# A transformer block in one kernel: four FFN halves computed inside the output projection, and a reordered compression

## The chip, the cores and the metric

The program runs on one core of one Trainium2 chip. The metric is the device time in microseconds, here the median of three runs. One further execution was taken by the hardware profiler, and all rows below are of that one.

## What is computed

One layer on 2048 tokens of width 1024: a mixer with three kinds of attention (one of them with compressed keys and values), an output projection, and a gated FFN with a short convolution. The parts that the change touches:

```python
def compress(a, pos, w1, b1, w2):            # a: keys or values, n T G hd
    ch = a.reshape(n, T // CMP_STRIDE, CMP_STRIDE, G, hd)
    blocks = jnp.concatenate([ch[:, j:j + nc] for j in range(n_sub)], axis=2)
    blocks = blocks + pos[None, None, :, None, :]
    flat = blocks.transpose(0, 1, 3, 2, 4).reshape(n, nc, G, CMP_LEN * hd)
    return jax.nn.gelu(flat @ w1 + b1) @ w2

mix = jnp.concatenate([o_a, o_b, o_c], axis=-1) @ w_out[l]
x = x + rmsnorm(mix, g_mix_post[l])
f = conv_glu_ffn(rmsnorm(x, g_ffn_pre[l]), w_up[l], conv_w[l], conv_b[l], w_down[l])
x = x + rmsnorm(f, g_ffn_post[l])

def conv_glu_ffn(h, w_up, conv_w, conv_b, w_down):
    u = causal_conv3(h @ w_up, conv_w) + conv_b      # per channel, 3 taps
    a, b = jnp.split(u, 2, axis=-1)
    return (jax.nn.gelu(a, approximate=True) * b) @ w_down
```

(`causal_conv3` stands for the grouped convolution of the reference.)

## The kernel before

The kernel is written engine by engine: each stage is a block in which every engine has its own list of instructions, with semaphores between them, and a stage begins when all engines have ended the one before. The stages are `project` (the input projection), `compress`, `attend`, `mix_out` (the output projection) and `ffn`. Nothing is scheduled by a planner; the order on each engine is the order of the code.

Every float32 product is made of three: an operand is split into a high part (a copy in the type float32r, made by ScalarE) and a low part (the difference, made by VectorE or GpSimd), and high × high, low × high and high × low are summed in one PSUM bank.

`compress` (L546) does this for m = 0 (keys) and m = 1 (values), each with a 2048 × 256 weight in 16 chunks, in quarters of 4 chunks. ScalarE makes `x_hi` (L656) and then `w_hi` per quarter (L659). VectorE makes the small low parts of the positions (L693), then `x_lo` (L683), then the low part of the weights in place in `w_raw` (L687). TensorE (L620 to L637) waits for `x_lo` and the first quarter's low part and goes chunk by chunk, with all three products of a chunk for both column halves. GpSimd only clears three tiles.

`mix_out` (L1531) goes over 16 row blocks of 128 tokens. In step t TensorE transposes the attention output of row block t + 1 (`turn_o`, L1749, into the PSUM tile `t1`), multiplies row block t by the output weights (L1767, tile `mix`, two slots) and transposes the normalised rows `h2` of row block t − 1 (L1776, tile `t2`). The last step, t = 16, has only the transposes of row block 15. SyncE's queue serves this in one fixed order, per step: three pieces of the attention output for t + 2 (`load_o`, L1601 to L1603), after the row block's `x1` is done its store (L1622) and the load of x for s + 2 (L1624), after the split of `h2` its two stores (L1627). Steps 0 and 1 are written out, the rest stands in a hardware loop (`steps`, L1580). When four row blocks are stored, GpSimd loads the FFN's first activations `f_h` (L1649, two loads of 2048 KB). Before the steps, ScalarE, VectorE and GpSimd split the output weights (L1640, L1654), whose raw rows lie in tiles of the attention stage (`w_rows`).

`ffn` (L1790) goes over four quarters of 512 tokens. In each, 22 steps `up` (L1895) make two halves each (b = 0, 1), a half being 24 matmuls (L1909) into one bank; ScalarE (L1954, L1955, L1959, L1961) and VectorE (L1992 to L2007) convolve, apply gelu and split the result. Then 22 steps `down` (L1913, L1929) fill all eight banks, and the row blocks are normalised and stored (VectorE L2013, L2018, GpSimd L1855 to L1867). The weights, 66 pairs of 512 KB per quarter, pass through a ring of 6 slots (SyncE, L1845, L1846); a slot is loaded again when TensorE is done with it. `up` waits for its slot, and for the banks that ScalarE has to empty:

```python
pe.wait_ge(w_in[s % RING], q * (32 * (STEPS // RING)) + 32 * (s // RING) + 32)
if j < 2:
    pe.wait_ge(f_taken, q * TQ + j + 1)
else:
    pe.wait_ge(u_done, q * (2 * NF) + 2 * (j - 2) + b + 1)
    pe.wait_ge(acc0_done, q * (2 * NF) + 2 * (j - 2) + b + 1)
```

All quarters are one hardware loop on each of TensorE, ScalarE, VectorE and SyncE.

## Time and profile before

| | us |
|---|---|
| median of 3 runs (3561.64 to 3566.04) | 3562.96 |
| the profiled execution | 3558.06 |
| its span, first to last instruction | 3556.3 |

| engine | busy us | share of the span |
|---|---|---|
| TensorE, matmuls | 3398.8 | 96% |
| TensorE, weight loads | 2708.3 | 76% |
| VectorE | 1385.9 | 39% |
| ScalarE | 1161.9 | 33% |
| GpSimd | 559.2 | 16% |

The span is what lies between the first and the last instruction of the profiled execution; that execution's own time is 1.8 us longer. The mean granted TensorE clock is 0.981 of full speed. DMA moved 190 GB/s in the mean. By the stages that matter here, the compression's TensorE work lies at 804 to 832 us from the span's start, the output projection at 1823 to 2049, and the FFN from 2058 to the end. A matmul's busy time in the rows overlaps with the next one's, so durations of many matmuls are read from their starts. Between `<-` and the name in square brackets a row says what ended an engine's idle time; "issue" is time in which it waited for nothing that the profile shows.

### The profile page before, as it was taken

To read this page: it belongs to the slowest core of one execution; us is meant where nothing else is said; L and a number is where in the kernel's file an instruction comes from. 1 tells how busy PE (TensorE), PEld (TensorE's weight loads), DVE (VectorE), ACT (ScalarE), POOL (GpSimd) and SP (SyncE) were. 2 spreads that over 40 slices of the span, in tenths; PEclk is the share of its full clock that TensorE was granted. 3 is DMA by queue.
4 is the path that set the end of the run, shared out by engine and by line. 5 is a ranking of instruction groups with operands and counts; after the bars stand their busy time and mean duration, and the time that the engine had idled before them with its cause. 6 is when DMAs were issued, how large, how long until landed. Compare 5 with 4: busy or idle time off the path is not lost. (4 is left out here: it accounts for less than half of the span.)

```text
span 3556.3 us, 45432 instructions
## 1 busy us (share of the span) xinstructions
PE 3398.8 (96%) x16530; PEld 2708.3 (76%) x16530; DVE 1385.9 (39%) x3826; ACT 1161.9 (33%) x1980; POOL 559.2 (16%) x487
## 2 busy tenths in 40 slices
PE   8999999997998999999989979999999999999997
PEld 6888888876777866666657768887888788878886
DVE  5111101105767766666644434403440254115421
ACT  5111111114666745554533323302330133013310
POOL 1566655420000013231010000000000000000000
PEclk9999999998999999999989989999999999999999
DMA  5788965667879622431237665566556655665553
GB/s 191 265 304 318 322 239 192 208 199 175 196 189 222 161 64 72 97 81 35 72 92 236 188 232 197 193 236 230 196 190 236 232 194 190 237 230 192 193 189 118
DMA packets 298533, 676.18 MB, mean 190 GB/s; under 512 B 99184, under 2 KB 154992, under 8 KB 283888
## 3 DMA queue, kind: packets, MB, share of 16 engines
q1 hardware_dynamic: 265616, 517.93, 45.8%
q0 software_dynamic: 32704, 155.40, 12.1%
q8 instruction: 135, 2.21, 0.3%
q14 instruction: 78, 0.64, 0.1%
HBM read 496.06 MB, written 185.57 MB: 192 GB/s over the span
## 5 line engine op out<-in xcount | busy, mean ns | idle before, releaser
L1909 PE MATMUL f_banks<-low,f_w_hi 128*128 128x512 f32 x2816 | 872.0, 390 | 28.7 <-DMA f_w_lo<-f_lo 20.0
L1909 PEld LDWEIGHTS f_banks<-low,f_w_hi 128*128 128x128 f32 x2816 | 530.8, 188 | 142.0 <-issue 25.6
L1909 PE MATMUL f_banks<-low,f_w_lo 128*128 128x512 f32 x1408 | 549.6, 390 | 0.0
L1267 PE MATMUL a_ot_ps<-a_turned_w,a_vs 128*65 128x256 f32 (+3 forms) x1452 | 449.7, 421 | 1.2 <-issue 1.2
L526 PE MATMUL z_banks<-h_hi,z_w_hi 128*128 128x512 f32 x972 | 387.2, 398 | 0.0
L526 PE MATMUL z_banks<-h_lo,z_w_hi 128*128 128x512 f32 x972 | 384.4, 396 | 0.0
L526 PE MATMUL z_banks<-h_hi,z_w_lo 128*128 128x512 f32 x972 | 384.3, 395 | 0.0
L1909 PEld LDWEIGHTS f_banks<-low,f_w_lo 128*128 128x128 f32 x1408 | 265.3, 188 | 55.0
L1340 ACT ACTIVATE w_small<-w_small,a_negm 128x128 f32<-128x128 f32 (+3 forms) x510 | 247.5, 518 | 166.2 <-DVE a_negm L1419 101.9
L1929 PE MATMUL f_banks<-f_w_hi,f_g_hi 128*128 128x512 f32 x704 | 278.4, 396 | 0.0
L1929 PE MATMUL f_banks<-f_w_hi,f_g_lo 128*128 128x512 f32 x704 | 278.4, 396 | 0.0
L1929 PE MATMUL f_banks<-f_w_lo,f_g_hi 128*128 128x512 f32 x704 | 278.4, 395 | 0.0
L1267 PEld LDWEIGHTS a_ot_ps<-a_turned_w,a_vs 128*65 128x65 f32 x1452 | 179.6, 139 | 82.6 <-issue 70.1
L1419 DVE CUSTOM_DVE_ANT_0 w_small<-a_s_ps,near 128x128 f32<-128x128 f32 (+2 forms) x456 | 169.5, 394 | 172.3 <-PE a_s_ps L1231 147.2
L526 PEld LDWEIGHTS z_banks<-h_lo,z_w_hi 128*128 128x128 f32 x972 | 182.6, 188 | 44.2
L526 PEld LDWEIGHTS z_banks<-h_hi,z_w_lo 128*128 128x128 f32 x972 | 182.7, 188 | 42.7
L526 PEld LDWEIGHTS z_banks<-h_hi,z_w_hi 128*128 128x128 f32 x972 | 182.8, 188 | 42.4
L2013 DVE SCALAR_TENSOR_TENSOR f_y<-f_banks,vk,f_gp 128x1024 f32<-128x1024 f32 x16 | 20.5, 1284 | 495.2 <-POOL vk L1862 494.8
L1242 PE MATMUL a_t_ps<-a_idt,w_small 128*128 128x128 f32 x1092 | 212.4, 278 | 0.0
L310 ACT ACTIVATE st_hi<-z_banks 128x512 fp32r<-128x512 f32 (+1 forms) x100 | 59.8, 598 | 461.3 <-PE z_banks L526 336.0
L445 DVE TENSOR_TENSOR st_lo<-z_banks,st_hi 128x512 fp32r<-128x512 f32 x76 | 52.4, 691 | 396.8 <-ACT st_hi L310 318.1
L1326 ACT ACTIVATE a_turned_w<-a_t_ps 128x512 f32<-128x512 f32 (+3 forms) x255 | 138.7, 549 | 199.2 <-PE a_t_ps L1242 198.5
(213 smaller groups left out, 5300.2 us busy)
## 6 DMA issues: line engine op xcount, KB each, us to landing
f_w_hi<-f_hi SPq DMA_DIRECT2D x264, 512.0 KB, 3.6
f_w_lo<-f_lo SPq DMA_DIRECT2D x264, 512.0 KB, 4.5
z_xs<-in_w_ffn POOLq DMA_DIRECT2D x33, 1024.0 KB, 8.4
f_hi<-z_v_hi POOLq DMA_DIRECT2D x33, 1024.0 KB, 4.9
f_lo<-z_xs POOLq DMA_DIRECT2D x33, 1024.0 KB, 5.7
low<-z_hi SPq DMA_DIRECT2D x48, 512.0 KB, 7.2
z_hi<-st_hi SPq DMA_DIRECT2D x84, 256.0 KB, 4.2
z_lo<-st_lo SPq DMA_DIRECT2D x84, 256.0 KB, 5.1
```

The costliest lines, as they stand in the source:

```text
L310: act.activation(out.bitcast(F32) if is_value(j) else out, bank, ACT.Copy).then_inc(zhi_done, 1)
L445: dve.tensor_tensor(low, bank, high, ALU.subtract).then_inc(zlo_done, 1)
L526: last = pe.matmul(banks[:, 4 * k + n, :], w[:, k, c, :], h[:, c, tok], start=(c == 0 and q == 0), stop=(c == DC - 1 and q == 2))
L1242: ins = pe.transpose(t_ps[:, b % TB, i, :], weights(n)[:, x * P:(x + 1) * P], idt[:])
L1267: last = pe.matmul(ot_ps[0:out_width(g), at:at + count * P], values, rows, start=(x == 0), stop=(x == len(blocks) - 1), skip_group_check=True)
L1326: ins = eng.activation(out, src, ACT.Copy) if e == 0 else eng.tensor_copy(out, src)
L1340: act.activation(weights(n), weights(n), ACT.Exp, bias=negm[:, n % 32:n % 32 + 1], scale=-1.0)\
L1419: dve.tensor_tensor_reduce(weights(n)[:, a:z], s_ps[:, c % SB, 0:z - a], table[:, at + a:at + z], -0.125, floor, ALU.add, ALU.min, low).th ...
L1909: last = pe.matmul(banks[:, bank, :], w[:, s % RING, c * P:(c + 1) * P], h[:, c, :], start=(c == 0 and x == 0), stop=(c == DC - 1 and x == 2))
L1929: last = pe.matmul(banks[:, 2 * t + n, :], g[:, d, tok], w[:, s % RING, cols], start=(d == 0 and x == 0), stop=(d == NF - 1 and x == 2))
L2013: dve.scalar_tensor_tensor(out=y[:], in0=banks[:, 2 * t:2 * t + 2, :].rearrange("p b n -> p (b n)"), scalar=rstd[:, t:t + 1], in1=gp[:], o ...
```

## The change

It has three parts.

1. **Compression.** GpSimd splits quarter 0 of the keys' weights, high and low, before it clears its tiles; ScalarE and VectorE begin with quarter 1. TensorE takes all 8 matmuls high × high of a quarter (4 chunks × 2 column halves), then the 8 with the weights' low part, then the 8 with the inputs' low part, and waits for each kind on its own. It starts when `x_hi` and the first quarter's high part are there.
2. **FFN row blocks.** The weight slots 0 to 3 of the ring now lie in tiles that outlive the attention stage (`k0_hi`, `k0_lo`, `qm`, `vs`), and SyncE loads them, and the convolution's constants, in `mix_out` between step 1 and the loop. After step 15 TensorE computes the halves 0 and 1 (j = 0), then makes the last transposes of `h2`, then the halves 2 and 3 (j = 1). PSUM is one tile `banks` for both stages. `y`, `h2` and `x1t` take the place of raw weight rows, for which VectorE and SyncE get a wait for the split of the output weights.
3. **FFN.** In each quarter TensorE's loop body begins at j = 2 and ends with j = 0 and 1 of the next; the last quarter is written out behind the loop. SyncE loads four slots ahead by the same counts. `y` lies in `acc[:, 1]`, for which ScalarE gets a wait at j = 1. The ring keeps 6 slots.

The core of the diff:

```diff
@@ compress
         @blk.gpsimd
         def _(pool):
+            first = w_hi[:, 0, quarter(0)]
+            raw = w_raw[:, 0, quarter(0)]
+            pool.wait_ge(w_in[0], 16)
+            pool.tensor_scalar(first, raw, 1.0, 1.0, ALU.mult, ALU.mult).then_inc(first_hi, 1)
+            pool.wait_ge(first_hi, 1)
+            pool.tensor_tensor(raw.bitcast(F32R), raw, first.bitcast(F32), ALU.subtract).then_inc(first_lo, 1)
...
-                pe.wait_ge(xlo_done, G * m + G)
-                for c in range(CMP // 2):
-                    if c % 4 == 0:
-                        pe.wait_ge(wlo_done, 4 * m + c // 4 + 1)
-                    for half in range(2):
...
+                pe.wait_ge(xhi_done, G * m + G)
+                for part in range(4):
+                    if m == 0 and part == 0:
+                        pe.wait_ge(first_hi, 1)
+                    else:
+                        pe.wait_ge(whi_done, 4 * m + part)
+                    for q, (w, x) in enumerate(((w_hi, x_hi), (w_raw.bitcast(F32R), x_hi), (w_hi, x_lo))):
+                        if q == 1 and m == 0 and part == 0:
+                            pe.wait_ge(first_lo, 1)
+                        elif q == 1:
+                            pe.wait_ge(wlo_done, 4 * m + part)
+                        elif q == 2 and part == 0:
+                            pe.wait_ge(xlo_done, G * m + G)
+                        for half in range(2):
+                            cols = slice(half * P, (half + 1) * P)
+                            for c in range(4 * part, 4 * part + 4):
+                                last = pe.matmul(hid[:, 2 * m + half, 0:G * NW], w[:, m, c, cols], windows(x, m, c),
...
@@ mix_out, SyncE
-            steps(sp, step)
+            first_steps(step)
+            sp.wait_ge(whi_done, DC)
+            for e in range(2):
+                sp.wait_ge(wlo_done[e], DC // 2)
+            for i in range(AHEAD):
+                load_ring(sp, ring, ring_in, f_hi, f_lo, i, i)
+            sp.dma_start(conv[:, :, 0:3], conv_w).then_inc(c_in, 16)
+            sp.dma_start(conv[:, :, 3], conv_b).then_inc(c_in, 16)
+            other_steps(sp, step)
+            step(NT, 0, NT // 2, False, NT)
@@ mix_out, VectorE, before its steps
+            dve.wait_ge(whi_done, DC)
+            for e in range(2):
+                dve.wait_ge(wlo_done[e], DC // 2)
@@ mix_out, TensorE
-            steps(pe, step)
+            first_steps(step)
+            other_steps(pe, step)
+            pe.sem_inc(pe_done, RING)
+            pe.wait_ge(h_in, 32)
+            pe.wait_ge(ring_in[0], 32)
+            pe.wait_ge(ol_done, NT)
+            up_half(pe, banks[:, 0, :], ring[0], f_h, pe_done)
+            pe.wait_ge(ring_in[1], 32)
+            up_half(pe, banks[:, 1, :], ring[1], f_h, pe_done)
+            step(NT, 0, NT // 2, False, NT)
+            pe.wait_ge(y_done, NT - 1)
+            for b in range(2):
+                pe.wait_ge(ring_in[2 + b], 32)
+                up_half(pe, banks[:, 2 + b, :], ring[2 + b], f_h, pe_done)
@@ ffn, SyncE
-            with sp.Fori(0, NQ) as q:
-                for s in range(STEPS):
-
-                    sp.wait_ge(pe_done, q * STEPS + s + 1)
...
+            def load(q, s):
+
+                sp.wait_ge(pe_done, q * STEPS + s + AHEAD + 1)
+                load_ring(sp, ring, ring_in, f_hi, f_lo, (s + AHEAD) % STEPS, s + AHEAD)
+
+            with sp.Fori(0, NQ - 1) as q:
+                for s in range(STEPS):
+                    load(q, s)
+            for s in range(STEPS - AHEAD):
+                load(NQ - 1, s)
@@ ffn, TensorE
-            with pe.Fori(0, NQ) as q:
-
-                pe.wait_ge(h_in, q * 32 + 32)
-                for j in range(NF):
+            def rest(q):
+                for j in range(2, NF):
                     up(q, j)
                 for d in range(NF):
                     down(q, d)
+
+            with pe.Fori(0, NQ - 1) as q:
+                rest(q)
+                pe.wait_ge(h_in, q * 32 + 64)
+                for j in range(2):
+                    up(q + 1, j)
+            rest(NQ - 1)
@@ ffn, ScalarE
                         act.wait_ge(gt_done, n + 1)
+                        if j == 1:
+                            act.wait_ge(out_done, q * TQ)
```

The first place is SyncE's queue in `mix_out` behind step 1; `p_ot` is the attention output of a row block. Before:

```order
L1627 DMA h_hi<-p_hh 1024x1x128
L1627 DMA h_lo<-p_hl 1024x1x128
L1584 UNCONDITIONAL_BRANCH
L1584 ISA
L1601 ISA
L1601 DMA p_ot<-o_heads 128x6x64
```

With the change:

```order
L1665 DMA h_hi<-p_hh 1024x1x128
L1665 DMA h_lo<-p_hl 1024x1x128
L1551 DMA k_hi<-f_hi 128x1024
L1551 DMA k_hi<-f_lo 128x1024
L1551 DMA k_lo<-f_hi 128x1024
L1551 DMA k_lo<-f_lo 128x1024
L1551 DMA qm<-f_hi 128x1024
L1551 DMA qm<-f_lo 128x1024
L1551 DMA vs<-f_hi 128x1024
L1551 DMA vs<-f_lo 128x1024
L1674 DMA vk<-in_conv_w 128x2x66
L1675 DMA vk<-in_conv_b 128x2x22
```

Ten transfers stand between the stores of row block 0 and the load of the attention output for row block 4, which follows.

The second place is TensorE's order from the last matmuls of `mix_out` to the FFN's first. Before:

```order
L1767 MATMUL p_mix<-p_w_lo,p_oh 128x512
L1776 MATMUL p_t<-p_idt,p_h 128x128 x16
L1533 UNCONDITIONAL_BRANCH
L1891 UNCONDITIONAL_BRANCH
L1935 UNCONDITIONAL_BRANCH
L1935 ISA
L1899 ISA
L1902 ISA
L1909 MATMUL f_banks<-low,f_w_hi 128x512
```

With the change:

```order
L1817 MATMUL banks<-p_w_lo,p_oh 128x512
L1826 MATMUL banks<-p_idt,w_small 128x128 x8
L1559 MATMUL banks<-low,k_hi 128x512 x24
L1559 MATMUL banks<-low,k_lo 128x512 x24
L1826 MATMUL banks<-p_idt,w_small 128x128 x8
L1559 MATMUL banks<-low,qm 128x512 x24
L1559 MATMUL banks<-low,vs 128x512 x24
L1567 UNCONDITIONAL_BRANCH
L1951 UNCONDITIONAL_BRANCH
L1995 UNCONDITIONAL_BRANCH
L1995 ISA
L1962 ISA
```

Four groups of 24 FFN matmuls stand around the last 8 transposes (of `h2`, now in `w_small`), ahead of the change of blocks.

## Rows read from the trace of the kernel before

**Rows 1.** Page, first line; the chain that ended last: start us, us, what.

```profile
span 3556.3 us, 45432 instructions
...
2060.15 9.15 DMA f_w_lo<-f_lo
...
2464.92 212.43 PE f_banks L1909 x936
```

**Rows 2.** TensorE, projection's end: start, us, engine, line, op [idle before <-releaser].

```profile
2038.19 1.04 PE L1776 MATMUL p_t<-p_idt,p_h 128*128 128x128 f32 x8
...
2047.47 1.97 PE L1776 MATMUL p_t<-p_idt,p_h 128*128 128x128 f32 x8 [8.25 <-DVE p_h L1733]
...
2069.42 0.79 PE L1909 MATMUL f_banks<-low,f_w_hi 128*128 128x512 f32 x1 [19.99 <-DMA f_w_lo<-f_lo]
```

**Rows 3.** Timelines of VectorE and SyncE's queue, same stretch.

```profile
2046.13 1.28 DVE L1733 SCALAR_TENSOR_TENSOR p_h<-p_x1t,p_st,p_gf 128x1024 f32<-128x1024 f32 x1
...
2050.53 1.23 DVE L1736 TENSOR_TENSOR p_hl<-p_t,p_hh 128x1024 fp32r<-128x1024 f32 x1 [3.12 <-ACT p_hh L1694]
...
2058.19 0.62 SPq L1839 DMA_DIRECT2D f_conv<-in_conv_w  x1
2078.01 0.32 SPq L1845 DMA_DIRECT2D f_w_hi<-f_hi  x1
```

**Rows 4.** Timelines of VectorE and GpSimd where the compression ends and the attention begins.

```profile
832.03 0.29 DVE L708 COPY vk<-c_vc_ps 127x128 f32<-127x128 f32 x1 [0.17 <-PE c_vc_ps L647]
...
833.42 1.80 POOL L1121 MEMSET k_lo<- 64x2048 f32 x1 [36.08 <-POOLq L551]
```

**Rows 5.** Windows: stretch, length, busy us by engine, TensorE clock, DMA share, GB/s.

```profile
2069.40:2075.50 6.10, 6.08 (x14) 4.79 (x15) 0.00 (x0) 0.00 (x0) 0.00 (x0) 0.50 1.03 410
874.80:878.00 3.20, 3.20 (x17) 3.00 (x17) 1.33 (x6) 1.39 (x3) 0.00 (x0) 0.50 1.03 236
```

**Rows 6.** TensorE's timeline in the attention stage.

```profile
874.80 0.48 PE L1230 MATMUL a_s_ps<-low 128*128 128x128 f32 x1 [5.58 <-DMA low<-z_lo]
```

**Rows 7.** SyncE's queue and TensorE's timeline at the third row block of the projection.

```profile
1859.24 2.54 SPq L1601 DMA_DIRECT2D p_ot<-o_heads  x1
...
1862.62 0.38 SPq L1603 DMA_DIRECT2D p_ot<-o_heads  x1
...
1868.03 1.04 PE L1749 MATMUL p_t<-p_idt,p_ot 128*128 128x128 f32 x8
```

**Rows 8.** DMA issues (KB, us to landing) and timelines around the FFN's activation load.

```profile
low<-h_lo POOLq DMA_DIRECT2D x1, 2048.0 KB, 14.5
...
1911.69 6.62 SPq L1601 DMA_DIRECT2D p_ot<-o_heads  x1
1919.63 0.38 SPq L1603 DMA_DIRECT2D p_ot<-o_heads  x1
...
1923.42 1.09 PE L1749 MATMUL p_t<-p_idt,p_ot 128*128 128x128 f32 x8 [3.47 <-DMA p_ot<-o_heads]
```

**Rows 9.** DMA rate in 40 slices of the stretch 2055 to 2080.

```profile
GB/s 288 288 192 0 0 0 0 142 287 210 172 128 214 334 421 413 419 419 419 420 420 419 419 419 419 406 406 393 413 406 413 406 400 433 393 406 393 419 413 406
```

**Rows 10.** Timelines of TensorE and ScalarE in the compression.

```profile
804.21 0.56 PE L634 MATMUL c_hid<-c_x_hi,h_hi 128*128 128x260 f32 x1 [11.15 <-DVE h_lo L687]
...
800.79 3.88 ACT L659 ACTIVATE h_hi<-h_lo 128x1024 fp32r<-128x1024 f32 x4
```

**Rows 11.** VectorE and GpSimd splitting output weights; VectorE splitting compression weights.

```profile
1820.01 2.53 DVE L1640 TENSOR_TENSOR p_w_lo<-k_hi,p_w_hi 128x1024 fp32r<-128x1024 f32 x1 [1.92 <-ACT p_w_hi L1654]
...
1819.11 2.35 POOL L1640 TENSOR_TENSOR p_w_lo<-k_hi,p_w_hi 128x1024 fp32r<-128x1024 f32 x1 [6.81 <-ACT p_w_hi L1654]
...
L687 DVE TENSOR_TENSOR h_lo<-h_lo,h_hi x8: 1217/1230/1245, 802.8 to 814.9; 128x1024 fp32r<-128x1024 f32 x8
```

**Rows 12.** Boundary of the FFN's first quarters: TensorE's timeline; the chain's rows of VectorE.

```profile
2436.41 0.49 PE L1909 MATMUL f_banks<-low,f_w_hi 128*128 128x512 f32 x1 [1.32 <-issue]
...
2455.09 5.93 issue
```

More of the change, by code:

```diff
@@ L1528, in _, with load_ring, up_half, mix_out @@
                     finish((n - 9) // 4)
-def mix_out(nc, ident, o_heads, o_mid, w_rows, w_in, junk, x, g_post, g_ffn, x1, h2_hi, h2_lo, f_h, h_in):
+AHEAD = 4
+def load_ring(eng, ring, ring_in, f_hi, f_lo, s, count):
+    for tile, rows in zip(ring[count % RING], (f_hi, f_lo)):
+        eng.dma_start(tile.bitcast(F32), rows[s]).then_inc(ring_in[count % RING], 16)
+def up_half(pe, out, tiles, h, pe_done):
+    (w_hi, w_lo), (h_hi, h_lo) = tiles, h
+    for c in range(DC):
+        for x, (w, rows) in enumerate(((w_hi, h_hi), (w_lo, h_hi), (w_hi, h_lo))):
+            last = pe.matmul(out, w[:, c * P:(c + 1) * P], rows[:, c, :],
+                             start=(c == 0 and x == 0), stop=(c == DC - 1 and x == 2))
+    last.then_inc(pe_done, 1)
+def mix_out(nc, ident, o_heads, o_mid, w_rows, w_in, junk, x, g_post, g_ffn, x1, h2_hi, h2_lo, f_h, h_in,
+            f_hi, f_lo, ring, ring_in, pe_done, conv, conv_w, conv_b, c_in, banks):
     with ExitStack() as ctx:
@@ L1586, in steps @@
                     step(2 * i + k, k, i, False, False)
-            for t in range(NT - 2, NT + 1):
+            for t in range(NT - 2, NT):
                 step(t, t % 2, t // 2, False, t)
@@ L1787, with ffn @@
 TQ = QT // P
[L1790 removed]
+def ffn(nc, h2_hi, h2_lo, f_h, h_in, stat, f_hi, f_lo, ring, ring_in, pe_done, conv, c_in, banks, x1, g_post, out):
     with ExitStack() as ctx:
@@ L1795, in ffn @@
         h_hi, h_lo = f_h
-        w_hi = sb("w_hi", [P, RING, D], F32R)
-        w_lo = sb("w_lo", [P, RING, D], F32R)
-        conv = sb("conv", [P, 2, 4, NF])
+        own = sb("own", [P, RING - AHEAD, 2, D], F32R)
+        ring = ring + [(own[:, i, 0, :], own[:, i, 1, :]) for i in range(RING - AHEAD)]
         cw, cb = conv[:, :, 0:3], conv[:, :, 3]
@@ L1906, in up @@
                         pe.wait_ge(acc0_done, q * (2 * NF) + 2 * (j - 2) + b + 1)
[L1907 to L1911 removed]
+                    up_half(pe, banks[:, 2 * (j % 2) + b, :], ring[s % RING], f_h, pe_done)
             def down(q, d):
                 s = 2 * NF + d
[L1915 removed]
+                w_hi, w_lo = ring[s % RING]
+                pe.wait_ge(ring_in[s % RING], q * (32 * (STEPS // RING)) + 32 * (s // RING) + 32)
                 pe.wait_ge(glo_done, q * NF + d + 1)
```

100 lines of the change are left out of this document (46 added, 54 removed).

## The prediction

> **What bounds the kernel now.** I read the chain of waits first. At the end it is TensorE almost alone, broken where the FFN begins: a transfer of `f_w_lo` takes 9.15 us, and nothing runs beside it [rows 1]. Next, TensorE's timeline around that place: the last row block's matmuls and a transpose end at about 2039.2. TensorE then idles 8.25 us for `h2`, transposes for 1.97 us and idles 19.99 us until FFN matmuls begin at 2069.42 [rows 2]. So of the 30.2 us between 2039.2 and 2069.4, TensorE works 2. The timelines of the other engines say what fills them [rows 3]: VectorE has `h2` at 2047.41 and the low half of its transpose at 2051.76; the stores follow, and only at 2058.19 does SyncE begin the FFN. The third view is the window of the restart: the clock is granted at 0.50 (1.2 GHz) until 2075.5 [rows 5]. Last, the places that the change loads: SyncE's queue in the projection, the compression, the boundaries of the FFN's quarters.
>
> **FFN row blocks moved forward.** One half (24 matmuls) takes 212.43 × 24/936 = 5.45 us warm [rows 1], those 936 being 39 halves. The first half before was cold: 2069.42 to SyncE's next load at 2078.01, about 8.5 us [rows 2, 3], so a cold start costs 3.0. Halves 2 to 4 are warm (16.35), and the fifth began at 8.5 + 16.35 after 2069.42, at 2094.3.
> With the change TensorE goes on at 2039.2: two halves to 2050.1, in place of an idle 8.25. `h2` has been ready since 2047.41, so the last transposes come at 2050.1 and end, warm (1.04 as in the first of [rows 2]), at 2051.2, where they ended at 2049.4 before: everything behind them is 1.8 later. The stores thus allow the next block at 2058.2 + 1.8 = 60.0 (I leave out 2000). Halves 3 and 4 end at 2051.2 + 10.9 = 62.1, so TensorE now sets the block's end. A change of blocks takes 833.42 − 832.32 = 1.1 [rows 4], so the FFN begins at 63.2.
> There it does not go on at once. Slots 4 and 5 are loaded in the FFN only, and the fifth half needs slot 4. Before, the first pair landed 2069.3 − 2058.19 = 11.1 us after the block began [rows 1, 3], of which some 1.4 us were the two convolution loads, now made earlier. GpSimd's loads still compete. I take 9.1, between 7.5 (slot 4's 1.05 MB and GpSimd's 1.57 at the 420 GB/s of [rows 9] are 6.2, and 1.3 for issue and start) and 11.1. The fifth half begins at 72.3, cold again after 10 us of idleness, so the 3.0 appear on both sides: 94.3 − 72.3 = 22.0, less 3.0 = **−19.0 us** (bounds −17.0 and −20.6). ScalarE needs `u` and `acc` of half 1 only, a few us, which lie under the 9.1.
>
> **Loads brought forward: eight times 512 KB and the convolution's on SyncE's queue.** They stand ahead of the third step's `load_o(4)`. Before, SyncE issued its three pieces from 1859.24 to 1863.0, and TensorE used them at 1868.03, without idling [rows 7]; that leaves almost no slack. Now ten issues come first. At 0.5 to 0.7 us each, `load_o(4)` is reached at about 1865.5, behind 4.19 MB. At 420 GB/s [rows 9] these take 10.0 us, from about 1862.1 (the stores of `h2` ahead of them) to 1872.1. By bytes alone `load_o(4)` (512 KB of small pieces) lands some 2.7 us later, 1874.8: 6.8 late.
> The trace has one near relative: the FFN's activations, two loads of 2048 KB, the same bytes, on GpSimd's queue. There SyncE was held 6.62 us in one issue and TensorE idled 3.47 us; it resumed at 1923.42, 5.1 us after the hold ended at 1918.3 [rows 8]. If the hold here ends at 1872.1, TensorE resumes at 1877.2: 9.2 late. I take 8.0 between the two. Idleness of 5.58 us was enough for a clock of 0.50 behind it [rows 5, 6], so a cold start of 3.0 is added: **+11.0 us** (bounds +3.5, as in [rows 8] and warm, and +15, if the pieces need 3 us more and the convolution's loads 1).
> The Trainium skill, "DMA: Bandwidth & Descriptors", section "Queues, rings and completion order", says that a queue's descriptors are taken in ring order and that the DMA engines alternate only between queues. By this the small pieces get no share until the eight loads are through, which favours 6.8 to 9.2; with sharing as between two queues the price would be near the 3.5 of [rows 8]. That is the first rival.
>
> **Compression.** TensorE waited until 804.21 for the first low part of the weights, while ScalarE had finished the first inputs' high parts at 800.79 [rows 10]. With GpSimd splitting quarter 0 from 796.4 on, the eight high × high matmuls can start at about 800.9: −3.3. Against it: VectorE's split takes 1.23 us alone, but 2.53 beside GpSimd's [rows 11], that is, it starts only when GpSimd's 2.35 us instruction is over. Two such instructions on GpSimd reach 801.2. VectorE's splits of positions and inputs slip, TensorE starts near 801.7 and waits 0.4 more for the low inputs: −2.1. I take **−2.7** (bounds −1.5, −3.3). After that VectorE gives a quarter of the weights every 1.23 us [rows 11], less than TensorE's 24 matmuls on one take, so the reordered passes have their operands.
> The Trainium skill, "SBUF — State Buffer", section "SBUF: two separate sides", calls the port pair of VectorE and GpSimd an exclusive lock held for a whole instruction. By this rule −2.1 stands rather than −3.3; the 2.53 us agrees with it.
>
> **At nothing.** VectorE's and SyncE's new waits for the output weights' split: that split is over before SyncE gets there, and TensorE waits for the same parts in its first step. The shared `y` and `acc`: ScalarE's new wait at j = 1 is met, as j = 0 already needed VectorE behind its last `out_done`. TensorE's loop edge moves from between quarters to behind j = 1: before, it cost 1.32 idle [rows 12], five halves then ended at 2463.7, and the sixth started at 2464.92 when ScalarE was done [rows 1]. The edge lies in the same stretch, so the end stays. The cover is 1.2 + 1.32 = 2.5 us; a dearer edge would show.
>
> **Sum.** −19.0 + 11.0 − 2.7 = −10.7 us. The profiled execution took 3558.06 (span 3556.3), which gives 3547.4; it lies 4.9 under the median of the runs, 3562.96. Against that median I predict **3552.3 us**. Only differences over 0.2% (7.1 us) can be told from none.
>
> **Rivals.**
> A, the queue shares. TensorE idles 3.5 at `load_o(4)` and stays warm: −19.0 − 2.7 + 3.5 = −18.2, 3544.8. For it: [rows 8]. Against: those bytes came over another queue.
> B, the backlog comes back: `load_o(5)`, or the x and `h2` transfers behind it, is late too and a second cold stall of 11 follows: +0.3, 3563.3. For it: SyncE was held long at [rows 8], and there is almost no slack at [rows 7]. Against: while TensorE waits, the queue drains, and behind the idle of [rows 8] the trace has no second one.
> C, slower: the loop edge. VectorE's own edge at this very time costs 5.93 us [rows 12], TensorE's cost 1.32 when DMA was calmer. If TensorE's moved edge costs 5.93, it ends j = 1 at 2456.9, begins j = 2 at 2462.8 and its second half at 2468.3 in place of 2464.9: 3.4, and a clock fall of 3.0. Three boundaries (the last one runs into new code instead of back) give +19.2: +8.5 in all, 3571.5. It starts to cost above 2.5 us per edge and outweighs the gain above some 3.6 of loss per boundary. Against it: TensorE's edge was 1.3 each time.
> That the change doesn't do what it says I exclude: the order shows the four halves, and their weights have 170 us to land.
>
> **Chances.** Forecast 0.50 (own range 3548 to 3557), A 0.20, B 0.16, C 0.07, and 0.07 between them. Faster by over 0.2% (below 3555.8): most of the forecast (0.44), A, half of the rest: 0.69. Within 0.2%: its tail 0.06, B, some of the rest: 0.23. Slower: 0.08. The range reaches from 3542 (A with the short landing) to 3562: it leaves out C and most of B.
>
> **What would show it.** In the profile after: 96 FFN matmuls before and after the last transposes with gaps under 1 us; the fifth half some 9 us after the FFN's start at a clock of 0.50; one idle of about 8 us in front of the fifth `o` transpose, waiting for DMA, and none before the next; compression's first matmul near 801; 5 halves and then ScalarE at each quarter's boundary. The forecast is wrong if that idle is under 5 or repeats, if the fifth half starts within 5 us of the block, or if idleness at the quarters' boundaries grows.

## The result, and the profile after

| | median us | runs | profiled execution | its span |
|---|---|---|---|---|
| before | 3564.5 | 4 (3561.64 to 3569.39) | 3558.06 | 3556.3 |
| changed | 3542.0 | 4 (3540.64 to 3542.96) | 3542.78 | 3541.0 |

The ratio is 0.9935, with a 95% interval of 0.9918 to 0.9952. The kernel is 22.5 us faster by the medians. I had predicted 3552.3, that is 10.7 us faster, with 3548 to 3557 as its own range and, with the rivals, a range down to 3542. The sign is right; the size is less than half of what was measured. From profile to profile the span fell by 15.3 only. So there are two questions: where 15.3 came from instead of 10.7, and why the medians lie 7 us further apart than the two profiled executions. The second stays open; the experiments only exclude some answers.

First the restart of the FFN. TensorE's timeline of the changed kernel from the last row block of the output projection on (start us, duration, engine, line, operation, and in brackets the idle before it and what ended it):

```profile
2052.57 1.04 PE L1826 MATMUL banks<-p_idt,w_small 128*128 128x128 f32 x8
2053.36 5.75 PE L1559 MATMUL banks<-low,k_hi 128*128 128x512 f32 x24
2058.94 5.61 PE L1559 MATMUL banks<-low,k_lo 128*128 128x512 f32 x24
2064.39 1.04 PE L1826 MATMUL banks<-p_idt,w_small 128*128 128x128 f32 x8
2065.18 5.70 PE L1559 MATMUL banks<-low,qm 128*128 128x512 f32 x24
2070.72 5.60 PE L1559 MATMUL banks<-low,vs 128*128 128x512 f32 x24
2082.91 9.43 PE L1559 MATMUL banks<-low,f_own 128*128 128x512 f32 x31 [6.60 <-DMA f_own<-f_lo]
```

The 8.25 and most of the 19.99 us of idleness of [rows 2] are gone: four halves (96 matmuls) stand in their place, without a gap, and one idle of 6.60 is left. SyncE's queue beside it, and the chain of waits at the same place (start us, us, what):

```profile
2068.35 0.68 SPq L1665 DMA_DIRECT2D h_lo<-p_hl  x1
2077.34 0.33 SPq L1551 DMA_DIRECT2D f_own<-f_hi  x1
2077.71 0.43 SPq L1551 DMA_DIRECT2D f_own<-f_lo  x1
```

```profile
2077.71 4.97 DMA f_own<-f_lo
2082.68 0.24 issue
2082.91 221.85 PE banks L1559 x960
2304.76 120.97 PE banks L1983 x528
2425.74 21.77 PE banks L1559 x96
2447.51 2.44 issue
2449.95 219.83 PE banks L1559 x960
2669.78 120.97 PE banks L1983 x528
2790.75 21.77 PE banks L1559 x96
2812.52 2.65 issue
2815.17 219.84 PE banks L1559 x960
3035.02 116.78 PE banks L1983 x510
```

The FFN's block begins at 2077.2, and the fifth half's weights land 4.97 us after their issue. The first piece of 960 matmuls takes 2.0 us more than the later ones: that is the cold start. And there is something that I had not priced. Per matmul the second product takes 120.97/528 = 0.2291 us here, against 119.02/510 = 0.2334 before; the first product takes 219.83/960 = 0.2290, against 0.2270 in [rows 1]. The piece of before:

```profile
2311.90 119.02 PE f_banks L1929 x510
```

Second, the loads brought forward. SyncE's queue and TensorE's timeline at the row block that uses `load_o(4)`, to be held against [rows 7]:

```profile
1860.71 1.42 SPq L1551 DMA_DIRECT2D k_hi<-f_hi  x1
...
1866.48 0.45 SPq L1551 DMA_DIRECT2D vs<-f_lo  x1
...
1869.32 3.81 SPq L1640 DMA_DIRECT2D p_ot<-o_mid  x1
1873.31 0.38 SPq L1641 DMA_DIRECT2D p_ot<-o_heads  x1
```

```profile
1878.69 1.96 PE L1799 MATMUL banks<-p_idt,p_ot 128*128 128x128 f32 x8 [8.78 <-DMA p_ot<-o_heads]
...
1936.21 1.18 PE L1799 MATMUL banks<-p_idt,p_ot 128*128 128x128 f32 x8 [3.77 <-DMA p_ot<-o_heads]
```

SyncE is held 3.81 us in the middle piece, and the transposes come behind an idle of 8.78 and cold (1.96 us for eight, 1.04 in [rows 7]). The idle of 3.77 is the one of [rows 8], which was there before. Third, the compression (TensorE, GpSimd, VectorE), against [rows 10]:

```profile
801.90 2.07 PE L650 MATMUL c_hid<-c_x_hi,h_hi 128*128 128x260 f32 x8 [7.95 <-ACT c_x_hi L672]
```

```profile
797.37 1.03 POOL L618 TENSOR_SCALAR h_hi<-h_lo 128x1024 fp32r<-128x1024 f32 x1 [30.75 <-POOLq L78]
798.48 2.37 POOL L620 TENSOR_TENSOR h_lo<-h_lo,h_hi 128x1024 fp32r<-128x1024 f32 x1
```

```profile
797.94 2.95 DVE L709 TENSOR_TENSOR c_x_lo<-poss,c_x_hi 128x24 fp32r<-128x24 f32 x4 [2.50 <-ACT c_x_hi L680]
800.81 4.01 DVE L699 TENSOR_TENSOR c_x_lo<-h_hi,c_x_hi 128x1024 fp32r<-128x1024 f32 x2
```

VectorE's four tiny splits (24 columns each) fill 2.95 us, and it goes on at 800.81, when GpSimd's 2.37 us instruction is over: it was held, as in [rows 11].

Put together, the two profiled executions differ by stage as follows. The marks are the first `k_lo` clear of the attention ([rows 4]: 833.42, after: 831.59), the first transposes of the output projection (1823.00, 1824.90), the end of the transposes of row block 14 (2039.22, 2053.61), the end of half 44 (2311.9, 2304.8), and the end.

| stage | before | after | difference | predicted |
|---|---|---|---|---|
| up to the attention | 833.4 | 831.6 | −1.8 | −2.7 |
| attention | 989.6 | 993.3 | +3.7 | 0 |
| output projection, to the transposes of block 14 | 216.2 | 228.7 | +12.5 | +11.0 |
| from there to the end of the quarter's 44 halves | 272.7 | 251.2 | −21.5 | −19.0 |
| the rest | 1244.4 | 1236.2 | −8.2 | 0 |

The first line holds a start that is 0.9 later, in a stage in which nothing was changed; the compression itself, from its first instruction on GpSimd to the attention's, takes 34.2 us instead of 37.0: −2.8.

### The profile page after: what moved, and what is told of

Same layout as the page of the kernel before. It is cut to its first block and busy times, and to the rows that moved or that the text cites. A ratio compares the mean times of both kernels' runs of the same rounds, so it can differ in the third digit from the quotient of the medians.

```text
span 3541.0 us, 45314 instructions
## 1 busy us (share of the span) xinstructions
PE 3398.4 (96%) x16530; PEld 2709.6 (77%) x16530; DVE 1386.2 (39%) x3825; ACT 1160.1 (33%) x1979; POOL 561.8 (16%) x489
## 3 DMA queue, kind: packets, MB, share of 16 engines
q0 software_dynamic: 32704, 155.40, 12.2%
## 5 line engine op out<-in xcount | busy, mean ns | idle before, releaser
L1281 PE MATMUL a_ot_ps<-a_turned_w,vs 128*65 128x256 f32 (+3 forms) x1452 | 450.1, 421 | 1.2 <-issue 1.2
L1559 PE MATMUL banks<-low,f_own 128*128 128x512 f32 x1344 | 319.4, 397 | 12.5 <-DMA f_own<-f_lo 6.6
L1559 PEld LDWEIGHTS banks<-low,f_own 128*128 128x128 f32 x1344 | 254.4, 190 | 73.3 <-issue 14.1
L1281 PEld LDWEIGHTS a_ot_ps<-a_turned_w,vs 128*65 128x65 f32 x1452 | 179.8, 139 | 83.1 <-issue 70.5
L2074 DVE SCALAR_TENSOR_TENSOR f_acc<-banks,vk,f_gp 128x1024 f32<-128x1024 f32 x16 | 20.5, 1284 | 482.8 <-POOL vk L1922 482.4
L1244 PE MATMUL a_s_ps<-low 128*128 128x512 f32 (+3 forms) x384 | 186.2, 488 | 6.6 <-DMA low<-z_lo 5.6
L1559 PE MATMUL banks<-low,k_hi 128*128 128x512 f32 x768 | 179.6, 389 | 0.0
L1559 PE MATMUL banks<-low,k_lo 128*128 128x512 f32 x768 | 179.3, 389 | 0.0
L2015 ACT ACTIVATE f_u<-banks 128x512 f32<-128x512 f32 x176 | 104.7, 595 | 215.0 <-PE banks L1559 214.9
L1559 PEld LDWEIGHTS banks<-low,k_hi 128*128 128x128 f32 x768 | 144.1, 188 | 30.4
```

The source lines that it names most:

```text
L1244: pe.matmul(out, query, hi[:, start + a:start + z], start=True, stop=False)
L1281: last = pe.matmul(ot_ps[0:out_width(g), at:at + count * P], values, rows, start=(x == 0), stop=(x == len(blocks) - 1), skip_group_check=True)
L1559: last = pe.matmul(out, w[:, c * P:(c + 1) * P], rows[:, c, :], start=(c == 0 and x == 0), stop=(c == DC - 1 and x == 2))
L2015: act.activation(u[:, k, b, 2:QT + 2], banks[:, 2 * k + b, :], ACT.Copy).then_inc(u_done, 1)
```

## Experiments

Eleven runs follow, in three lots, each on another chip: nine new kernels and the two known ones once more. The runs of before that accompanied them have medians of 3563.5 (19 runs), 3560.4 (9) and 3563.6 (9). Each ratio is to the runs of before in the same lot. The changed kernel itself ran in the first lot only (experiments 1 to 3), so a difference of 2 or 3 us between it and a kernel of the other lots (experiments 4 to 10) shows nothing by itself.

**1. The kernel before again, and the changed one again.** No edit. Labels `before_again` and `after_again`.

> The kernel before once more. The first profile of it took 3558.1 us, its four other runs 3561.6 to 3569.4, which is a spread of 8 us where the changed kernel has 2.3. Theory 1: the spread comes from the clock: short idle times of TensorE (1.0 to 2.5 us at the boundaries of the FFN's quarters and in the attention) are followed by a granted clock of 0.50 in some executions and not in others. This profile then differs from the first in how many such falls there are, about 1.7 us for each, and the stages without idle times agree within 0.5 us. Theory 2: the spread comes from DMA; then the falls are as many as before, and the boundaries of the quarters differ by the landing of out and x.

> The changed kernel once more, to separate what the change does from what differs between two executions. Its first profile lost 3.7 us against before in the attention, where nothing was changed but addresses, and won 4.2 us at the last boundary of the quarters. Theory 1 (chance): the attention differs by the places of the clock falls and comes out anywhere between -4 and +4 us of before. Theory 2 (the change): +3.7 in the attention and -4.2 at the last boundary again. The idle time before the fifth transpose of o is again 8 to 9 us, the fifth half again starts 5 to 6 us behind the change of blocks, the total is 3540 to 3544.

Measured: 3561.6 (8 runs, 3558.79 to 3566.69) and 3541.7 (4 runs, 3539.45 to 3543.31; ratio 0.9936, interval 0.9919 to 0.9953). The executions of before spread over 8 us and more (19 others from 3557.57 to 3572.85), those of the changed kernel over 4. The profiled execution of before lies near the bottom of its runs again: 3558.79. Span against span the difference is 3557.0 − 3540.5 = 16.5. The idle ahead of the fifth `o` transposes was 8.81 this time and that ahead of the fifth half 6.76, so both are no accident. This trace of before has the two idles at each of the FFN's boundaries too, but no fall of the clock there. By stage the second pair of traces differs as follows, in the order of the table above:

| stage | before again | changed again | difference |
|---|---|---|---|
| up to the attention | 835.4 | 831.2 | −4.1 |
| attention | 992.0 | 994.8 | +2.8 |
| output projection, to the transposes of block 14 | 217.4 | 227.1 | +9.7 |
| from there to the end of the quarter's 44 halves | 271.3 | 251.4 | −19.9 |
| the rest | 1241.0 | 1236.1 | −4.9 |

So a single pair of traces fixes a stage only to 1 to 3 us. Part of that is the restart of before: its 1056 matmuls, 239.7 us when warm, took 242.5 in the first trace (2069.42 to 2311.90) and 241.1 in the second (2074.92 to 2316.04). Neither pair of theories comes out clean. The attention of before took 2.4 us longer in this trace, with no more time at the lower clock, so falls of the clock are not what its executions differ by; and the change loses time in the attention again, but at the last boundary it wins 2.0 and not 4.2.

**2. The loads without the row blocks.** Everything as in the changed kernel, but all halves are computed in the FFN:

```diff
-            pe.wait_ge(ring_in[0], 32)
...
-            up_half(pe, banks[:, 0, :], ring[0], f_h, pe_done)
...
             step(NT, 0, NT // 2, False, NT)
...
+            for s in range(AHEAD):
+                pe.wait_ge(ring_in[s], 32)
+                up_half(pe, banks[:, s, :], ring[s], f_h, pe_done)
```

> The first four slots are loaded early as in the changed kernel, but all four halves are computed at the start of the FFN's block. Theory 1 (early loads and moved halves both pay): the halves no longer wait for a load, so the FFN starts about 11 us earlier against its block than before, but cold (8.5 us for the first half) and with 8.25 + 8 us idle ahead of it: the fifth half starts 14 to 15 us later than in the changed kernel, total 3556 to 3558. Theory 2 (the halves fill time in which TensorE had to wait for slot 4 anyway): then total at most 3548.

Measured: 3557.0 (10 runs, ratio 0.9981, interval 0.9969 to 0.9992), profiled 3554.8. TensorE's timeline:

```profile
2059.91 1.97 PE L1826 MATMUL banks<-p_idt,w_small 128*128 128x128 f32 x8 [8.25 <-DVE w_small L1783]
2070.98 4.54 PE L1559 MATMUL banks<-low,k_hi 128*128 128x512 f32 x10 [9.10 <-PEq L1567]
```

The 8.25 are back, and of the 19.99 of [rows 2] only 9.10 are: weights that have landed long before are worth some 11 us at the FFN's start, as much as it costs to load them there. Theory 1 holds. What makes the change pay is the computing in the gap: from the last transposes of block 14 to the end of the 44 halves this kernel takes 263.0 us and the changed one 251.2, which is 11.8; the spans differ by 12.0 and the medians by 15.0.

**3. The old compression in the changed kernel.**

```diff
-                pe.wait_ge(xhi_done, G * m + G)
-                for part in range(4):
...
+                pe.wait_ge(xlo_done, G * m + G)
+                for c in range(CMP // 2):
+                    if c % 4 == 0:
+                        pe.wait_ge(wlo_done, 4 * m + c // 4 + 1)
```

> The changed kernel with the compression as before. Theory 1 (the sum's term): 2.7 us slower than the changed kernel, all of it between the compression's block and the attention's: 37.0 us instead of 34.3. Theory 2 (the attention gives it back, since its first idle time waits for DMA): the same total within 1 us.

Measured: 3547.9 (4 runs), profiled 3546.28, that is 3.5 and 4.0 above the two profiled executions of the changed kernel. The stage takes 37.4 us in place of 34.2: 3.2. Nothing of it is given back in the attention, so theory 2 falls. By the medians the compression would be worth 6; the four runs of each kernel do not overlap, but the intervals of the two ratios (0.9940 to 0.9973 and 0.9919 to 0.9953) do, so I hold to what the stage itself shows, and the rest is open.

**4. The ring loads later.** SyncE issues the same ten transfers behind its loop:

```diff
             first_steps(step)
+            with sp.Fori(1, NT // 2 - 1) as i:
+                for k in range(2):
+                    step(2 * i + k, k, i, False, False)
             sp.wait_ge(whi_done, DC)
...
             sp.dma_start(conv[:, :, 3], conv_b).then_inc(c_in, 16)
-            other_steps(sp, step)
-            step(NT, 0, NT // 2, False, NT)
+            for t in range(NT - 2, NT + 1):
+                step(t, t % 2, t // 2, False, t)
```

> The eight ring loads and the two convolution loads are issued by SyncE behind its loop over steps 2 to 13 instead of ahead of it, everything else as in the changed kernel. Theory 1 (they cost what they do only because they stand ahead of load_o(4)): the idle of 8.8 us before the fifth o transpose and the cold start behind it vanish, output projection from first transposes to the end of step 15 takes 216 to 217 us instead of 228.7, the time is 11 to 12.5 us lower than the changed kernel's, 3529 to 3531. Theory 2 (the same 4.19 MB hurts wherever it stands): a wait of about the same size appears at step 14's or 15's load_o or at h2's stores, and the time is 3538 to 3543. Theory 3: the four halves find their weights late, since only some 25 us are left, and the restart gives back 3 to 8 us: 3533 to 3538.

Measured: 3531.6 (4 runs, 3528.77 to 3533.51; ratio 0.9916, interval 0.9898 to 0.9933). The idle ahead of the fifth transposes is gone. The stage from the first transposes to those of block 14 takes 216.0, what it took before (216.2). The loads' weights are in time for the halves, and the restart has the same shape:

```profile
2039.20 1.04 PE L1829 MATMUL banks<-p_idt,w_small 128*128 128x128 f32 x8
2040.00 5.75 PE L1559 MATMUL banks<-low,k_hi 128*128 128x512 f32 x24
...
2069.63 2.90 PE L1559 MATMUL banks<-low,f_own 128*128 128x512 f32 x6 [6.68 <-DMA f_own<-f_lo]
```

Theory 1 holds, with a time 0.6 above its range. The place of the loads cost 12.6 us by the profiles (1824.90 to 2082.91 against 1824.25 to 2069.63) and 10.4 by medians, which come from two lots.

**5. The ring loads on GpSimd's queue**, at the same time as in the changed kernel:

```diff
             split_lower(pool, 0, 0, DC)
...
+            pool.wait_ge(hl_done, 1)
+            for i in range(AHEAD):
+                load_ring(pool, ring, pool_in, f_hi, f_lo, i, i)
```

> The eight ring loads stand at the same time as in the changed kernel but on GpSimd's queue. Rival A of the prediction (DMA engines alternate between queues, so the small pieces of load_o(4) on SyncE's queue get their share): the idle before the fifth o transpose falls from 8.8 to 3.5 us or less, without a cold start, 5 to 9 us lower than the changed kernel: 3533 to 3537. The theory by bytes alone (the DMA engines work through 4.19 MB whatever the queue): idle stays 7 to 9 us and the time 3540 to 3543.

Measured: 3542.7 (4 runs, 3538.57 to 3543.97), the changed kernel's time. Timelines of SyncE's queue and of TensorE:

```profile
1867.70 7.47 SPq L1641 DMA_DIRECT2D p_ot<-o_mid  x1
1875.36 0.38 SPq L1642 DMA_DIRECT2D p_ot<-o_heads  x1
```

```profile
1880.68 1.54 PE L1802 MATMUL banks<-p_idt,p_ot 128*128 128x128 f32 x6 [8.71 <-DMA p_ot<-o_heads]
```

SyncE is held 7.47 us instead of 3.81 and TensorE waits 8.71 instead of 8.78. Against TensorE's matmuls, SyncE reaches `load_o(4)` 3.7 us earlier than in the changed kernel (the two loads for the convolution are still ahead of it), and yet the pieces land at the same time. They get no better share beside the large transfers than behind them. That settles rival A: it is not the order in one queue that makes `load_o(4)` late. The Trainium skill, "DMA: Bandwidth & Descriptors", section "Queues, rings and completion order", has the DMA engines go round between queues packet by packet; no gain from this is seen here for transfers of such small pieces. That alone does not speak against the turns: `load_o(4)` has 1536 pieces of 256 bytes and 128 of 1 KB, the eight loads together 1024 rows of 4 KB, so that turns in which a small piece waits for a large one would shelter it little (a reading of the shapes in the kernel, not tried). Why the issue is held so long is open.

**6. `g` at another address, in the kernel before.** Here the theory on the pace that I had not priced is tested. Each tile's start address in a partition of SBUF has a remainder by 512 bytes; the addresses are those of the built programs, no trace shows them. The activations `low`, and the weights `f_w` of before and the slots `k0`, `qm`, `vs` of the changed kernel have 416; the own slots `f_own` have 32; `g` has 480 before and 416 after. In both kernels the matmuls are slower exactly where the two operands' remainders differ: 5.44 us for 24 matmuls where they agree, about 5.6 where they don't.

```diff
+        g_hi = sb("g_hi", [P, NF, QT], F32R)
+        g_lo = sb("g_lo", [P, NF, QT], F32R)
         conv = sb("conv", [P, 2, 4, NF])
...
-        g_hi = sb("g_hi", [P, NF, QT], F32R)
-        g_lo = sb("g_lo", [P, NF, QT], F32R)
```

> The kernel before with g_hi and g_lo placed ahead of conv, at an address whose remainder by 512 bytes is the weights' own (416), where it was 480; nothing else changes. Theory of addresses (a matmul whose stationary and moving operand start at the same remainder by 512 takes 0.2269 us per 512 columns, otherwise 0.2333): every step of the FFN's second product goes from 5.60 to 5.44 us, 88 of them, about 14 us in all: 3548 to 3551. Rival (the pace of 5.60 belongs to the second product's own structure, eight banks written in turn): nothing changes, 3559 to 3565.

Measured: 3550.2 (6 runs, 3547.03 to 3554.05; ratio 0.9968, interval 0.9955 to 0.9981), 10.2 under before in the same lot. The chain's pieces of TensorE in the FFN:

```profile
2317.11 115.61 PE f_banks L1929 x510
2466.92 212.44 PE f_banks L1909 x936
```

The second product goes from 119.02 to 115.61, 0.2267 us a matmul, and the first stays at 212.44. The time lies in the range, the theory holds, and the rival on the structure of the second product falls. The pieces account for 3.4 × 528/510 × 4 = 14.1; this profile has two falls of the clock in the FFN, 1.5 us each, that the second trace of before has not, and the medians show 10.

**7. Own slots and `g` at the same remainder, in the changed kernel.** 384 bytes are left free ahead of the own slots, and `g` comes right behind them.

```diff
+        sb("gap", [P, 96])
         own = sb("own", [P, RING - AHEAD, 2, D], F32R)
+        g_hi = sb("g_hi", [P, NF, QT], F32R)
+        g_lo = sb("g_lo", [P, NF, QT], F32R)
```

> The changed kernel with its own two slots of weights moved by 96 words (remainder by 512 bytes 416 instead of 32) and g_hi, g_lo placed so that they stay at 416. Theory of addresses: halves and steps that read the own slots take 5.44 us instead of 5.58 to 5.60, about 88 of 264, so 12 to 13 us less than the changed kernel: 3529 to 3531. Rival (the own slots are slower because they are loaded while in use by TensorE, or because of their place in the order): unchanged, 3540 to 3543.

Measured: 3530.3 (4 runs, 3528.6 to 3532.54; ratio 0.9912, interval 0.9895 to 0.9930): 11.7 less by medians of two lots and 12.2 by the spans, for an edit that moves no instruction. The rival falls: the own slots are loaded and used in the same order as before.

```profile
2423.45 21.76 PE banks L1559 x96
2447.78 217.88 PE banks L1559 x960
2665.67 119.68 PE banks L1984 x528
```

960 take 217.88 instead of 219.83, and 528 take 119.68 instead of 120.97. Both products are at 0.2267 to 0.2270 a matmul now.

**8. TensorE's loop edge back between the quarters.** The four moved halves stay where they are.

```diff
-            with pe.Fori(0, NQ - 1) as q:
-                rest(q)
-                pe.wait_ge(h_in, q * 32 + 64)
-                for j in range(2):
-                    up(q + 1, j)
-            rest(NQ - 1)
+            rest(0)
+            with pe.Fori(1, NQ) as q:
+                pe.wait_ge(h_in, q * 32 + 32)
+                for j in range(2):
+                    up(q, j)
+                rest(q)
```

> The changed kernel with TensorE's loop over the FFN's quarters turned back: the edge lies between the quarters again, in front of j = 0, as before; the four halves of the first quarter stay in the output projection. Theory 1 (part of the gain and the kernel before's wider spread of 8 to 15 us come from its quarter boundaries, where TensorE idles 1.3 at the edge and 0.8 to 2.8 for ScalarE five halves later, which lets the clock fall at some boundaries and not at others): the two idles are back at all three boundaries, at least one clock fall of 3.4 us among them or a spread of 7 us or more over the runs, median 2 to 5 us over the changed kernel's 3542: 3544 to 3547. Theory 2 (the spread came from the long idle ahead of the FFN, which is gone here): spread 4 us, 3541 to 3544.

Measured: 3539.4 (5 runs, 3537.04 to 3541.8; ratio 0.9928, interval 0.9915 to 0.9942). My theory 1 fell; the time lies 1.6 under theory 2's range as well, which is less than lots differ by. The idles come back where the edge is, at the boundaries (TensorE's timeline, the second of them; at the first, which has no edge in this kernel, there is none of the first kind):

```profile
2786.67 5.71 PE L1559 MATMUL banks<-low,k_hi 128*128 128x512 f32 x24 [1.11 <-issue]
2815.80 5.83 PE L1559 MATMUL banks<-low,f_own 128*128 128x512 f32 x24 [1.50 <-ACT f_acc L2016]
```

But neither time nor spread follows. From the first quarter's first matmul of the second product to the last quarter's it takes 3395.22 − 2301.75 = 1093.5 us; in the changed kernel, with the edge behind j = 1, 3398.47 − 2304.76 = 1093.7, and in the kernel of experiment 5, with the same edge, 3399.57 − 2306.18 = 1093.4. So where the edge lies costs nothing, as predicted. That there are two edges instead of three, with one quarter written out, is common to both.

**9. Everything that helped.** The late loads; gaps so that operands agree in the projection (`z_w` at 192 before, `h` at 416), the output projection (`p_w` at 32, `oh`, `ol` at 64 in the changed kernel) and the FFN.

```diff
+        sb("gap", [P, 56])
         w_raw = sb("w_raw", [P, 2, DC, P])
...
+        keep.enter_context(nc.sbuf_tensor("gap", [P, 96], F32))
         with ExitStack() as mid:
...
-        eps = sb("eps", [P, 1])
...
+        eps = st[:, 0, 6:7]
```

> Late ring loads together with addresses: gaps are put in so that the stationary and the moving operand of the projection's, the output projection's and all FFN's matmuls start at the same remainder by 512 bytes (416). Theory of addresses: FFN 11.8 us less, as in the run that moved own slots and g alone; projection 2916 matmuls x 0.0064 = up to 18.7 less, if TensorE bounds it throughout; output projection 768 x 0.0056 = 4.3 less. From 3531.6: 3496 to 3502. Rival (the projection is paced by ScalarE's and VectorE's evictions and the weights' splits, so that only some of it is seen): 3503 to 3518.

Measured: **3496.1** (4 runs, 3494.38 to 3497.2; ratio 0.9806, interval 0.9791 to 0.9821). GpSimd's first instruction of the compression, which marks the projection's end, in the kernel with late loads alone and in this one:

```profile
796.77 1.03 POOL L618 TENSOR_SCALAR h_hi<-h_lo 128x1024 fp32r<-128x1024 f32 x1 [30.65 <-POOLq L78]
```

```profile
778.70 1.03 POOL L619 TENSOR_SCALAR h_hi<-h_lo 128x1024 fp32r<-128x1024 f32 x1 [28.86 <-POOLq L78]
```

The projection ends 18.1 earlier, 97% of what its 2916 matmuls at 0.0064 us give: TensorE bounds it almost throughout, and the rival falls. This kernel is 45.9 us under the changed one and 67.4 under before.

**10. The last wait too.** As experiment 9, and SyncE loads slots 4 and 5 already behind the last stores of `h2`, into the place of `y`, `h2` and a row of `x1`; its loads in the FFN begin two slots further on.

```diff
+            sp.wait_ge(h_turned, NT)
+            load_ring(sp, ring, ring_in, f_hi, f_lo, AHEAD, AHEAD)
+            sp.wait_ge(x1_out[0], 16 * (NT // 2 + 1))
+            load_ring(sp, ring, ring_in, f_hi, f_lo, AHEAD + 1, AHEAD + 1)
```

> As the last, and slots 4 and 5 of the FFN's weights are loaded by SyncE already in the output projection, behind the last h2 stores: they lie where y, h2 and the x1 row of step 14 were, which are free from the last transposes on. Theory: the idle of 6.6 us before the fifth half and its cold start of 1.9 vanish, TensorE waits some 1.5 to 2.5 us for ScalarE's first u and acc only: 5 to 7 us less than the run before it, 3490 to 3496. Rival (4 more transfers beside the last h2 stores delay the end of the output projection's block by as much): within 2 us of that run.

Measured: 3495.7 (4 runs, 3491.53 to 3497.94), within 0.4 of the run before it. The time is the rival's, but the mechanism is neither. TensorE, then ScalarE:

```profile
2046.32 7.15 PE L1560 MATMUL banks<-low,own 128*128 128x512 f32 x24 [3.80 <-ACT f_acc L2023]
2055.31 6.89 PE L1560 MATMUL banks<-low,own 128*128 128x512 f32 x22 [1.84 <-ACT f_acc L2023]
```

```profile
2043.61 1.28 ACT L2022 ACT_TABLE_LOAD   x1 [10.96 <-PEq L1568]
2044.90 0.60 ACT L2022 ACTIVATE f_u<-banks 128x512 f32<-128x512 f32 x1
2045.40 0.77 ACT L2023 ACTIVATE f_acc<-banks,vk 128x512 f32<-128x512 f32 x1
2046.19 1.28 ACT L2027 ACT_TABLE_LOAD   x1
2053.39 0.63 ACT L2027 ACTIVATE f_acc<-f_acc 128x512 f32<-128x512 f32 x1 [5.91 <-DVE f_acc L2068]
```

```profile
2051.54 0.17 DVE L2060 COPY f_u<-f_halo 128x2 f32<-128x2 f32 x1 [17.63 <-DMA f_gp<-in_g_ffn_post]
```

The fifth half waits for no weights any more but for ScalarE, which begins the FFN with a table load of 1.28 us; the sixth waits again, since ScalarE waits 5.91 for VectorE. VectorE's first instruction there comes at 2051.54, behind the load of `gp`, the weights of the last normalisation, for which VectorE waits ahead of all its work in the FFN though these instructions do not read them. My theory had this wait in it, but as 1.5 to 2.5 us where 3.80 and 1.84 came: under the transfer of slot 4 there lay a second wait of nearly its length. Whether an earlier load of `gp` would remove it wasn't tried.

## Why the prediction was right in sign and off in size

By the medians the kernel gained 11.8 us more than forecast. Three steps of the prediction failed. The rest of the FFN was put at nothing and gave −8.2 (in the second pair of traces −4.9). Slot 4 landed 3.4 us earlier than I took. And the difference of two profiled executions was taken for that of the medians, which lie 7.2 further apart. Against the first two stood 3.7 us lost in the attention, also put at nothing, 1.5 more for the loads and the start that was 0.9 later.

**FFN row blocks, −19.0 predicted.** The halves, the transposes between them and the end of the block (23.6 us behind row block 14's transposes, 24.0 predicted) came as worked out. The step that failed here is the landing of slot 4. I took 9.1 us from the start of the block, between 7.5 and 11.1; it was 5.7 (2077.2 to 2082.91), outside the bounds. The lower bound had GpSimd's 1.57 MB ahead of the 1.05 MB of slot 4, but SyncE's first pair was through after 4.97 us. That is −3.4. The cold start was 2.0 and not 3.0, another −1.0. The other way goes the pace: a third of the 40 halves that remain read the own slots, 13.3 × 0.14 = +1.9. Together with the 0.4 of the block's end: −19.0 − 3.4 − 1.0 − 0.4 + 1.9 = −21.9, against −21.5 in the first pair of traces. The −19.9 of the second pair has the same early landing in it; there the restart of before was 1.4 us faster.

**Loads brought forward, +11.0 predicted.** The idle was 8.78 for 8.0, between my two estimates, SyncE was held, the start was cold, and no second one followed. The stage grew by 12.5; taking the loads away from there gave back 10.4 (medians) to 12.6 (profiles). In the second pair the stage grew by 9.7. Right. My reason from the order within a queue was not what decides: experiment 5.

**Compression, −2.7 predicted.** 2.8 by the stage, 3.2 in experiment 3. The size is right, the way to it is not. TensorE starts 4.5 us behind GpSimd's first instruction of the stage (801.90 and 797.37), before it was 7.8 (804.21 and 796.43): 3.3 earlier, my outer bound. That 801.90 lies beside my 801.7 is luck, as the stage began 0.9 later. TensorE waited only for ScalarE's `x_hi`: GpSimd's high part took 1.03 us and not 2.35, and the low inputs were there in time, so that the further 0.4 of waiting didn't come. Of the 3.3 some 0.5 is lost again by the end of the stage. The lock of VectorE by GpSimd's instruction, which the Trainium skill describes in "SBUF — State Buffer", section "SBUF: two separate sides", shows again in the 2.95 us; it delayed VectorE, but not TensorE.

**At nothing.** I had checked waits and edges, not whether the same matmuls run at the same pace, nor that one edge less is passed.

- Moving tiles changed the pace: of three quarters and the last second product, the first product got slower by 1.95 a quarter and the second faster by 2.25, which makes 3 × 1.95 − 4 × 2.25 = −3.2 in "the rest".
- The boundaries: beyond the pace they took 2.6, 3.2 and 5.2 us before and 2.4, 2.7 and 0.9 after, −5.0 in all. The third is the quarter written out, which I had wrongly counted as an edge like the others; and in the kernel before it had a fall of the clock besides, from 3198.5 to 3201.9. In the other trace of before, without falls, they sum to 7.2, against 6.0 and 5.8 in the two traces of the changed kernel, so the change itself is worth 1 to 1.5. Of the other 3.8 us the fall explains 1.6, the rest differs between executions of before.
- The attention took 993.3 to 995.2 us in the ten traces of the changed kernel and its variants, and 989.6, 992.0 and 993.0 in the three of before and its variant. Part of it is granted clock: away from the stage's two ends TensorE is at its lower level for 20 to 24 us in the first and for 17 to 20 in the second, which is worth at most 3.5 us. The stage's instructions are the same, and three of its tiles that stay (`w_small`, `near` and the unit matrix) start at a remainder of 32 where it was 416. In experiments 9 and 10 they are back at 416 and the stage still takes 994.4 and 994.6, so their remainder alone doesn't explain it (other tiles of the stage moved in these two); the cause stays open.

**The medians.** I had assumed that the difference between two profiled executions is that between medians. Of before, both profiled executions and the first of each lot of accompanying runs lie between 3557.6 and 3559.1, and the medians near 3563; the changed kernel's profiled ones lie within 1 us of its median. So 6 to 7 of the 22.5 us are in executions of which there is no trace, nearly all of before. The wider spread is also in experiment 2 (12.6 us) and in part in experiment 6 (7.0), and not in experiment 8 (4.8), so it isn't the loop edge. Nor is it the mean granted clock: of the 19 executions in the first lot, those of 3557.92 and 3572.85 us both have 0.981, and 0.001 of it is worth only 3.6 us. The kernels with the spread have a long idleness ahead of the FFN, but the cause stays open.

**The rivals.** A is refuted by experiment 5, B by the absence of a second cold stall behind the one of 8.78, C by the edges themselves, 2.44 and 2.65 us where it wanted 5.93, and by experiment 8.

## What to carry to other kernels

When a change moves tiles, compare the time per matmul of each group of instructions that stays: here edits that only shift addresses were worth 11.7 us in the FFN and 18.1 in the projection, together more than the whole reordering of the FFN's start. Put prefetches where the queue has slack: the same ten transfers cost 10 us ahead of the loop and none behind it. And before removing the last wait at a stage's start, look for the second one beneath it, table loads of ScalarE included.

## What was not expected of the hardware

- A matmul with both operands in SBUF took 0.2267 to 0.2270 us per 512 columns where the two start addresses have the same remainder by 512 bytes, and about 0.233 where they had not (416 against 480, 416 against 32, 416 against 192), at full granted clock. A remainder by 256 would fit the cases seen as well, one by 128 would not (416 and 32 differ by 384). Operands whose remainders differ by 32 to 384 all had the slower pace. All pairs that agree here agree at 416; whether they must be equal, or must both be at 416, no run separates.
- 4.19 MB in large transfers held up a load of small pieces as much from another queue as from its own: TensorE waited 8.71 and 8.78 us for it.
- TensorE's loop edge cost 1.3 us between the quarters in the kernel before and 2.4 and 2.7 behind j = 1 in the changed one (2.2 to 3.4 in its variants), and yet the end is the same, since in the first case ScalarE's wait follows.
